# Map back by streams and narrow router logits in a four-layer diffusion backbone

## What is computed

```
for l in range(4):                    # mixers: Fourier, attention, gated MLP, Mamba scan
    mp, ms = adaln(c_ctx), adaln(c)   # six rows of 1024 for each stream: silu(cond) @ ada_w[l] + ada_b[l]
    o  = mixer(modulate(rmsnorm(h, norm1_g[l]), m, 0)) @ w_out     # "map back" is this @ w_out
    h  = h + m[2] * o
    t  = modulate(rmsnorm(h, norm2_g[l]), m, 3)
    g  = softmax(t @ w_gr + b_gr)     # 4 groups: take the best one
    e  = t @ w_er + b_er              # 16 experts: top 2 of the 4 in that group
    h  = h + m[5] * sum over the 2 experts of  w * ((silu(t @ w_gate) * (t @ w_up)) @ w_down)
```

## Time and profile before

| | |
|---|---|
| time, median of 3 runs | 1865.47 us (1863.54 to 1865.65) |
| time of the profiled execution | 1858.52 us |
| its span, first to last instruction | 1856.7 us |
| mean granted TensorE clock, as a share of full speed | 0.973 |
| PE / PEld busy | 1752.8 us (94%) / 930.6 us (50%) |
| DVE / ACT / POOL busy | 526.8 / 364.6 / 101.9 us |
| moved by DMA | 614.10 MB, mean 331 GB/s |

### The profile page before, as it was taken

How to read it: one execution, slowest core, us unless ns; L and a number is a source line. 1 busy time by engine, 2 the same in 40 slices (tenths; PEclk the granted TensorE clock), 3 DMA queues, 4 the chain that set the end, 5 groups by cost and what they waited for, 6 DMA issues and landing times.

```text
span 1856.7 us, 20922 instructions
## 1 busy us (share of the span) xinstructions
PE 1752.8 (94%) x8794; PEld 930.6 (50%) x8794; DVE 526.8 (28%) x1149; ACT 364.6 (20%) x671; POOL 101.9 (5%) x171
## 2 busy tenths in 40 slices
PE   5999999999999999999999999999999999899995
PEld 2554444376544444334855444336786654634441
DVE  1131121310631212220032121224245882212123
ACT  2131111111421111121102111013223651201111
POOL 1000000000000000000000000000003740000000
PEclk8989999999899999999998999999999999799998
DMA  9999999997279999899456899998854656499991
GB/s 401 358 401 429 427 429 428 400 353 291 98 284 381 428 428 428 359 371 343 170 195 266 367 429 427 428 377 307 323 174 155 172 194 238 185 429 427 429 428 70
DMA packets 92850, 614.10 MB, mean 331 GB/s; under 512 B 7504, under 2 KB 7728, under 8 KB 51408
## 3 DMA queue, kind: packets, MB, share of 16 engines
q1 hardware_dynamic: 85584, 585.36, 77.5%
q0 software_dynamic: 7168, 27.33, 4.7%
HBM read 608.34 MB, written 4.33 MB: 330 GB/s over the span
## 4 chain that ended last, share of the span: by engine, by line
PE 85%; DVE 5%; DMA 4%; ACT 3%; issue 2%; POOL 0%; SPq 0%; DVEq 0%; ACTq 0%; POOLq 0%
PE psum L1024 23%; PE psum L590 15%; PE psum L583 12%; PE psum L1059 12%; PE psum L1006 6%; PE psum L1075 6%; PE psum L641 4%; DMA ring<-in_fnet_w_o 2%; PE psum L975 1%; DMA ring<-in_moe_w_down 1%; DMA ring<-in_ada_w 1%; DVE arena L1704 1%; PE psum L1044 1%; PE psum L921 1%; ACT arena L1369 1%
## 5 line engine op out<-in xcount | busy, mean ns | idle before, releaser
L1024 PE MATMUL psum<-ring,arena 128*64 128x512 f32 x1152 | 343.0, 594 | 0.0
L583 PE MATMUL psum<-at,ring 128*128 128x256 f32 x1024 | 223.6, 380 | 0.0
L583 PEld LDWEIGHTS psum<-at,ring 128*128 128x128 f32 x1024 | 194.2, 190 | 28.0 <-issue 1.6
L1024 PEld LDWEIGHTS psum<-ring,arena 128*64 128x64 f32 x1152 | 108.0, 137 | 165.2 <-issue 165.2
L1024 PE MATMUL psum<-arena 128*64 128x512 f32 x608 | 190.0, 594 | 0.0
L1768 DVE TENSOR_TENSOR outtmp<-psum,gate 128x512 f32<-128x512 f32 x128 | 87.7, 685 | 345.9 <-PE psum L1075 345.9
L1059 PE MATMUL psum<-ring,arena 128*64 128x512 f32 x624 | 183.1, 593 | 0.0
L590 PE MATMUL psum<-ring,at 128*128 128x512 f32 (+1 forms) x416 | 172.3, 570 | 0.4 <-DVE at L1622 0.4
L1075 PE MATMUL psum<-arena 128*128 128x512 f32 x256 | 117.6, 603 | 25.0 <-ACT arena L1369 15.0
L1759 DVE TENSOR_TENSOR arena<-arena,psum 128x512 f32<-128x512 f32 x32 | 34.0, 1062 | 356.7 <-PE psum L1024 356.7
L590 PE MATMUL psum<-ring,arena 128*128 128x512 f32 x288 | 125.7, 596 | 0.6 <-DMA ring<-in_fnet_w_o 0.6
(11 more groups left out here) (249 smaller groups left out, 1595.2 us busy)
## 6 DMA issues: line engine op xcount, KB each, us to landing
ring<-in_ada_w SPq DMA_DIRECT2D x43, 2048.0 KB, 10.4
ring<-in_moe_w_down SPq DMA_DIRECT2D x39, 2048.0 KB, 17.5
ring<-in_moe_w_up SPq DMA_DIRECT2D x38, 2048.0 KB, 14.2
ring<-in_moe_w_gate SPq DMA_DIRECT2D x34, 2048.0 KB, 16.7
arena<-in_moe_w_gate SPq DMA_DIRECT2D x22, 2048.0 KB, 12.2
arena<-in_moe_w_down SPq DMA_DIRECT2D x17, 2048.0 KB, 16.3
arena<-in_moe_w_up SPq DMA_DIRECT2D x16, 2048.0 KB, 14.5
ring<-in_ssd_w_in SPq DMA_DIRECT2D x12, 2048.0 KB, 10.5
```

Source lines behind the costliest of these rows:

```text
L583: last = nc.tensor.matmul(dst, slot(k)[:, c, m * P:(m + 1) * P], src[:, c, :], start=(c == 0), stop=(c == nk - 1))
L1024: last = nc.tensor.matmul(ps[b][e * CAP:(e + 1) * CAP, :], rows, slot_half(k + e, 4, h)[:, c, :], start=(h == 0 and c == 0), stop=(h == 1 ...
```

## The change

Four things change.

- In layers 2 and 3 the map back goes stream by stream (`map_part`): both column halves of stream 0, then those of stream 1. `slot_done` for a block is raised by stream 1's use. In layers 2 to 4, stream 0's eight transposes stand before stream 1's second half, and DVE and ACT modulate stream 0 there (`stream_modulated` between the third and fourth addition, `stream_scaled` after each stream's root).
- The logits become two steps for each stream. `stream_logits`: the router weights, padded with zeros from 20 to 32 columns, are stationary and 128 tokens move; the eight blocks of 128 channels go to four column tiles (32 columns each), two to a tile. DVE copies the 128x128 result to `parts` (`parts_copied`), and one matmul with the matrix `fold` sums the four tiles and turns the result back to tokens (`stream_folded`, 20 columns).
- Between map back and experts the order of PE in layers 2 and 3 is: logits 0, two conditioning slots, fold 0, transposes of stream 1, tokens 0, logits 1, fold 1, tokens 1, the third slot, positions, `gather(0)`, the fourth slot with its bias. In layer 4 the same without slots. In layer 1 both streams go together as before, with the new logits, then three slots, and the fourth after `gather(0)`.
- `ada_turned` and DVE's `modulation` of the next layer move to behind the first pair's up product, ACT's `ada_evicted` to behind the first gather's copies. At the start DVE zeroes the padding of `wr` and makes `fold`.

The core of the diff (declarations and bank numbers left out):

```
-            def out_proj(n, src, halves):
+            def map_part(n, s, j, kk, src, halves):
+                k = AT[n, f"O{j * halves + kk}"]
+                arrive(k)
+                if n == 2 and s == 0:
+                    pe.wait_ge(sp_ev, SG // 2 * (kk + 1))
+                last = dense_tok(k, s, ps[out_bank(n, j, s)][:, :], src, kk * DC, DC, kk == 0, kk == halves - 1)
+                if s:
+                    last.then_inc(slot_done, 1)
+                elif kk == halves - 1:
+                    last.then_inc(o_mm, 1)
...
+            def stream_logits(n, s):
+                pe.wait_ge(at_act, S * (2 * n + 1) + s + 1)
+                pe.wait_ge(at_dve, S * (2 * n + 1) + s + 1)
+                for r in range(2):
+                    for g in range(4):
+                        last = nc.tensor.matmul(ps[4][LOGITS * g:LOGITS * (g + 1), s * P:(s + 1) * P], wr[:, LAYERS[n], 4 * r + g, :],
+                                                at[:, 4 * r + g, s * P:(s + 1) * P], start=(r == 0), stop=(r == 1))
+                last.then_inc(parts_mm, 1)
+            def stream_folded(n, s):
+                pe.wait_ge(parts_ev, S * n + s + 1)
+                nc.tensor.matmul(bank(5, S, NR)[:, s, :], parts[:, s, :], fold[:, 0:NR], start=True, stop=True).then_inc(route_mm, 1)
...
-                    out_proj(n, oT, 1)
+                    map_part(n, 0, 0, 0, oT, 1)
+                    map_part(n, 0, 1, 0, oT, 1)
+                    map_part(n, 1, 0, 0, oT, 1)
+                    stream_turned(n, 1, 0)
+                    map_part(n, 1, 1, 0, oT, 1)
...
+                    stream_logits(n, 0)
+                    if n < 3:
+                        for q in range(2):
+                            ada_slot(n, f"A{n + 1}.0.{q}")
+                    stream_folded(n, 0)
+                    stream_turned(n, 1, 1)
+                    stream_tokens(n, 0)
+                    stream_logits(n, 1)
+                    stream_folded(n, 1)
+                    stream_tokens(n, 1)
+                    if n < 3:
+                        ada_slot(n, f"A{n + 1}.0.2")
...
-                if n < 3:
-                    ada_turned(n + 1, 0)
...
                 gather(0)
                 if n < 3:
-                    pe.wait_ge(mod_ready, 3 * (n + 1) + 1)
+                    ada_slot(n, f"A{n + 1}.0.3")
...
                     else:
+                        if n < 3:
+                            ada_turned(n + 1, 0)
                         gather(1)
```

More of the change, by code:

```diff
@@ L48 @@
 CAP = 64
+LOGITS = 32
 PAIRS = E // 2
@@ L182, in build @@
         gscs = [sb(f"gsc{i}", [P, 2, DC, S]) for i in range(2)]
-        wr = sb("wr", [P, DEPTH, DC, NR])
+        wr = sb("wr", [P, DEPTH, DC, LOGITS])
+        parts = sb("parts", [P, S, P])
+        fold = sb("fold", [P, LOGITS])
         rbias = sb("rbias", [P, DEPTH, NR])
@@ L672, in ada_after, with stream_turned @@
                     ada_slot(n, w)
+            def stream_turned(n, which, s):
+                pe.wait_ge(xn_ready, S * (2 * n + which) + s + 1)
+                for h in range(2):
+                    for c in range(4):
+                        last = nc.tensor.transpose(bank(2 * s + h, 4, P)[:, c, :],
+                                                   xn[:, s, (4 * h + c) * P:(4 * h + c + 1) * P], mat("ident"))
+                    last.then_inc(tr_mm, 1)
             def norm_transposes(n, which):
-                t = 2 * n + which
                 for s in range(S):
[L679 to L684, removed]
+                    stream_turned(n, which, s)
                     if n and which == 0:
@@ L843, in _ @@
                         last.then_inc(sp_mm, 1)
-                    out_proj(n, uT, 2)
+                    for kk in range(2):
+                        for j in range(2):
+                            map_part(n, 0, j, kk, uT, 2)
+                    for j in range(2):
+                        if j:
+                            stream_turned(n, 1, 0)
+                        for kk in range(2):
+                            map_part(n, 1, j, kk, uT, 2)
                 else:
@@ L970, in _ @@
[L970 to L983, removed]
@@ L997, in gather @@
+                nc.tensor.matmul(bank(4, S + 1, E)[:, 2, :], mat("ones"), sel16[:, 1, :], start=False, stop=True).then_inc(pos_mm, 1)
                 def gather(x):
@@ L1188, in norm_scaled, with stream_scaled @@
-            def norm_scaled(n, which):
+                    stream_stats(n, which, s)
+            def stream_scaled(n, which, s):
                 t = 2 * n + which
                 act.wait_ge(gsc_ready, 2 * n + which + 1)
-                for s in range(S):
[L1193 to L1197, removed]
+                act.wait_ge(tr_mm, 4 * t + 2 * s + 1)
+                for c in range(4):
+                    last = A(at[:, c, s * P:(s + 1) * P], bank(2 * s, 4, P)[:, c, :], ACT.Identity,
+                             scale=gscs[n % 2][:, which, c, s:s + 1], bias=modts[n % 2][:, 3 * which * DC + c, s:s + 1])
+                last.then_inc(at_act, 1)
@@ L1199, in _, with norm_scaled, stream_tokens @@
+            def norm_scaled(n, which):
+                for s in range(S):
+                    stream_scaled(n, which, s)
+            def stream_tokens(n, s):
+                for h in range(2):
+                    act.wait_ge(tok_mm, 4 * n + 2 * s + h + 1)
+                    A(xn[:, s, :].rearrange("p (c q) -> p q c", c=DC)[:, h * 64:(h + 1) * 64, :],
+                      ps[2 * s + h].rearrange("p (q c) -> p q c", c=DC), ACT.Copy).then_inc(tok_ev, 1)
             for n, l in enumerate(LAYERS):
@@ L1357, in _ @@
                     A(rt[:, 2 + 5 * r, :, :], rt[:, 1 + 5 * r, :, :], ACT.Exp).then_inc(rexp, 1)
[L1358 to L1362, removed]
+                if n == 0:
+                    stream_tokens(n, 0)
+                stream_tokens(n, 1)
                 def gathered(x):
@@ L1496, in add_mixer @@
                     V.tensor_tensor(hid[:, s, cols], hid[:, s, cols], outtmp[:, i % 2, :], ALU.add).then_inc(h_ready, 1)
+                    if n and i == 2:
+                        stream_modulated(n, 1, 0)
+                    if n and i == 3:
+                        parts_copied(n, 0)
                     if j == 1:
@@ L1576, in _ @@
                         norm_scale(0, s)
+                    V.memset(wr[:, :, :, NR:LOGITS], 0.0)
+                    V.tensor_reduce(fold[:, :], mat("ident").rearrange("p (g i) -> p i g", g=P // LOGITS), AX.X, ALU.add).then_inc(fold_ready, 1)
                     modulation(0, 0)
-                modulate(n, 0)
+                for s in range(S):
+                    stream_modulated(n, 0, s)
                 if l == 0:
@@ L1801, in _ @@
                     activated(x)
+                    if x == 0 and n < 3:
+                        modulation(n + 1, 0)
                     if x:
```

133 lines of the change are left out of this document (77 added, 56 removed).

## The result

| kernel | median, lowest to highest (runs) | ratio to before, 95% interval |
|---|---|---|
| before | 1865.39 us, 1863.02 to 1867.52 (6) | 1 |
| changed | 1853.39 us, 1851.99 to 1858.22 (6) | 0.9947 (0.9934 to 0.9959) |

The change makes the kernel 12.0 us faster. The changed kernel's profiled execution took 1851.99 us (span 1850.2, granted clock 0.978), 6.5 us less than the profiled execution before.

The account below looks back on a forecast made before the run. PE, 85% of the chain, was taken to bound the kernel. Layers 1 to 4 summed as 0 + 0.6 - 1.0 - 3.5 = -3.9 us, put on the median 1865.47: 1861.6 us, range 1857.0 to 1868.0.

Parts of the forecast that it names:

- A logits call: New tiled logits, one stream: 16 records at 0.55 us, bounded by 0.53 and 1.79; 1.1 at half clock.
- The gather of layer 2: Layer 2, after the route: gather starts at 557.25 instead of 562.65, 5.4 us gained.
- that of layer 3: Layer 3, after the route: gather starts at 1017.1 instead of 1024.11, 7.0 us gained.
- The slot, bias and turning behind it: Layers 2 and 3: work leaving the route's shadow for behind the gather gives back 3.9 us in each.
- The price of half clock in the two gathers: Gathers of layers 2 and 3 fall to half clock after idle times: 2.1 us each, bounds 0 and 3.35.
- Layer 1 gives nothing: Layer 1: shorter logits only lengthen the sixth down product's wait for weights, 0 us, at most 0.7.
- Rival D: A logits call costs a slot's 1.79 us, double at half clock: 7.5 us more, some 1869.1 us; chance 0.13.
- C: The weight stream takes the gains of layers 2 to 4: no change, about 1865.2 us; chance 0.13.
- the last line of the sum: Terms from the 1858.52 us profiled execution are differences, so -3.9 us goes on the median 1865.47: 1861.6 us.
- Rival B: The clock does not fall, or falls where PE waits anyway: -8.1 us in all, 1857.4 us; chance 0.27.
- Layer 4: Layer 4, map back to gather: route starts at 1586.3 instead of 1589.91; 3.5 us faster after 0.1 for longer idling.
- Layers 2 and 3: Net of gather gains, work behind the gather and half clock: layer 2 +0.6 us, layer 3 -1.0 us.

Follow-up runs that it names:

- shadow kernel: The changed kernel with the fourth conditioning slot back ahead of the position products and the turning ahead of the gather in layers 2 and 3: 1845.96 us, 0.9908.
- second profile of before: The kernel before, unchanged, run and profiled again: ratio 1.0003 to before, span 1863.4 us in the new profile.
- fill_before: The kernel before with nothing else changed but useless 128x128 products in PE's idle times in layers 2 to 4: 1851.49 us, 0.9922.
- the two filled kernels: Useless products in PE's idle times, added to the kernel before (1851.49 us, 0.9922) and to the changed kernel (1849.76 us, 0.9921).
- Logits alone: The kernel before with the tiled logits, copy and fold, in the old order, each call waiting for its own stream only: 1849.19 us, 0.9921.
- streams-only kernel: The kernel before with the order by streams and late fourth slot and turning, but logits of 20 columns, one call per stream: 1860.24 us, 0.9985.

## Why the prediction was wrong

**The steps of the schedule held.** A logits call was priced at 0.55 us and took 0.65, 1.08 at half clock (1.1). Copy and fold took the 0.29 and 0.40 that were put down; a hand-over took some 0.05, not 0.15. The gather of layer 2 comes 6.3 us earlier, counted from the start of the map back (forecast 5.4), that of layer 3 7.9 (7.0). The slot, bias and turning behind it cost 3.5 in each, as the shadow kernel shows (forecast 3.9). The price of half clock in the two gathers came true as well: 1.4 and 2.7 us, 4.1 together, for the 4.2 put down. Layer 1 gives nothing: the end of the map back of layer 2 lies between 538.9 and 545.5 whatever logits layer 1 has, and the down block's wait grew. Rival D is out (a call is far from 1.2 us), and so is C for layers 2 to 4: no wait on a transfer stands in their expert stages.

**The failed step is the last line of the sum, "all terms are differences, so they go on the median", and behind it the clock of the kernel before.** The forecast took one execution of before as the kernel. The differences were differences to an execution 6.9 us under its median, while the profiled execution after is 1.4 under its own. That makes 5.5 of the 8.1 us by which the forecast fell short. What the runs show in its place: the kernel before itself loses time at half clock, a different amount in each execution (50.1 us in the first profile, 57.8 in the second, by span times (1 minus clock)), and the change takes part of that loss away. So the 2.1 us charged in layer 2 were not all a loss that the change brings. In the second profile of before, and in that of the kernel with layer 4 alone changed, layer 2's gather takes 5.44 us in the old order, too; layer 3's takes 3.81 in all three.

The other 2.6 lie between the two profiles: the gains of layers 2 and 3, expert stages included, are 1.9 and 1.1 larger than forecast, that of layer 4 is 2.2 larger, and 2.6 go off because the part ahead of layer 2 came out longer in that execution, 1.8 of it ahead of layer 1's conditioning slots, where the waits for the first conditioning blocks were longer (11.3 us in all against 7.2).

Rival B (no clock loss, 1857.4) comes nearer in its number only: its condition, gathers that stay at 3.8 us, did not hold. As a bound, span times (1 minus clock) is what half clock would cost if PE worked all through it: 57.8 us in the median of before, 44.4 in the changed kernel, 39.8 with filler in the kernel before. Clock times span meanwhile goes from 1805.3 to 1807.5 and 1809.3. So by this split the whole gain is clock and none of it is schedule; since PE also idles at half clock, the true share is smaller, and how much smaller stays open. That clock alone can give such a gain without any shortening is shown by fill_before; the two filled kernels side by side leave the shorter way, at full clock, no gain that stands out of their intervals.

**Layer 4** was mis-sized (3.5 forecast, 7 alone, 5.7 between the profiles). Between the profiles, 4.3 lie behind the map back, net of the transposes: the forecast kept 3.51 us from stream 1's transposes to its logits, and it took 2.77; fold and hand-overs were 0.5 shorter; the position products fell to half clock and took 0.7 back. The other 1.4 lie ahead of it, where the mixer of the kernel before has a stretch at half clock (0.51 from 1530.80 to 1534.10) that the changed kernel's profile lacks at that place; no edit touches this stretch. **Layers 2 and 3** had 0.4 forecast and give some 3.4 between the profiles, 6 alone. The rest of the 6, like that of layer 4's 7, may be the reference again, since those are ratios to the median of before; no run separates it.

**What was not seen:** order by streams, as built, is a loss beside the new logits, though not by itself (0.9985, 0.9974 to 0.9996). Logits alone are 4 us faster than the whole change. Order by streams opens an idle time in front of the position products and pushes 3.5 us of work behind the gather in each of two layers; with that work back in the shadow, it costs nothing (1846.0 us, logits alone 1849.2, intervals that overlap). The prediction had both numbers, but did not ask which part earns what.

## What to carry to other kernels

Before a term worth a few microseconds is read from a profile, compare that execution's time with the median and its granted clock with that of the other runs: the profiled one may be the kernel at its luckiest, and what looks like a loss that the change brings may be one that the kernel already pays. Where PE waits between short, narrow instructions, put work there that has to be done anyway, and if there is none, useless products that fit the gap; here that alone was worth no less than the whole change (15 and 12 us). Price the parts of a change apart, since a good part can carry one that loses.

## What was not expected of the hardware

- 44 useless 128x128 products in PE's idle times made the kernel 0.78% faster (0.9906 to 0.9938), and brought 20-column logits from 6.99 to 3.81 us by the clock alone.
- Executions of one kernel without any change differ by up to 12 us (1856.54 to 1868.28), and the granted clock goes with it (0.974 to 0.967); which stretches fall to half clock changes from one execution to the next: layer 2's first gather took 3.81 us in one profile and 5.44 in another.
- Eight matmuls in four column tiles of 32 took 0.65 us where the same logits of one stream, with 20 columns moving, took 1.86 in the streams-only kernel (16 records): 2.9 times. No gap stands at the change of tile shape: the slots follow the call without idle time.
